# A layer's second output as seven block products with weight sums made in memory

## The reference, cut to what matters

```
h = rmsnorm(x, norm_ffn2) * (1 + sc3) + sh3
a, b = split(h @ w_in)            # w_in: 1024 x 5632
x = x + 0.5 * gt3 * (silu(a) * b) @ w_out     # g = silu(a) * b: 640 x 2816, w_out: 2816 x 1024
y = rmsnorm(x, norm_final)
```

## Time and profile before

| | |
|---|---|
| runs (us) | 1293.56, 1292.83, 1290.88 |
| profiled execution | span 1290.3 us; the page gives no whole time for it |
| TensorE busy | 1271.7 us of the span, 8909 matmuls |
| VectorE, ScalarE, POOL busy | 929.5, 553.6, 99.9 us |
| granted clock of TensorE | 0.999 of full in the mean |
| moved by DMA | 170.02 MB, mean 132 GB/s |

### The profile page before, as it was taken

The page is one execution under the profiler, slowest core; times in us unless marked ns, Lnnn a source line. Parts: engine busy times, 40 slices in busy tenths (PEclk is TensorE's granted clock), DMA queues, the critical chain, the costliest instruction groups (busy, mean ns, idle before and its releaser), DMA issues.

```text
span 1290.3 us, 23138 instructions
## 1 busy us (share of the span) xinstructions
PE 1271.7 (99%) x8909; PEld 1221.2 (95%) x8909; DVE 929.5 (72%) x1537; ACT 553.6 (43%) x920; POOL 99.9 (8%) x81
## 2 busy tenths in 40 slices
PE   9999999999999999999999999999999999999998
PEld 7889999999999999999999899999999999988886
DVE  5668877787887864666899867557988877771424
ACT  6514543445532224664433554336544343451223
POOL 0000000000000000002433663000000000000000
PEclk9999999999999999999999999999999999999999
DMA  9771423232476745348864552242243423274222
GB/s 372 296 271 31 117 78 98 69 94 63 142 219 189 217 119 142 89 116 192 246 201 100 146 157 83 66 71 78 66 129 97 142 72 98 65 185 103 71 83 98
DMA packets 238101, 170.02 MB, mean 132 GB/s; under 512 B 46305, under 2 KB 209606, under 8 KB 236998
## 3 DMA queue, kind: packets, MB, share of 16 engines
q1 hardware_dynamic: 234964, 165.51, 43.2%
q0 software_dynamic: 1440, 2.62, 1.5%
q10 hardware_dynamic: 1618, 0.81, 0.2%
HBM read 154.32 MB, written 19.83 MB: 135 GB/s over the span
## 4 chain that ended last, share of the span: by engine, by line
PE 80%; DVE 8%; DMA 5%; issue 3%; ACT 2%; POOL 2%; SPq 0%; POOLq 0%; DVEq 0%; ACTq 0%
PE ps L1043 32%; PE ps L850 26%; PE ps L1473 11%; PE ps L1420 3%; DMA d_ex<-d_gc 2%; PE ps L973 1%; DMA w_raw<-in_w_ffn_in 1%; PE ps L1406 1%; DVE cv L2513 1%; DVE w_lo L2109 1%; DVE sub_tmp L2633 1%; DMA cw_raw<-in_w_ada 1%; DVE pn L2178 1%; PE ps L918 1%; POOL Rc L3054 1%
## 5 line engine op out<-in xcount | busy, mean ns | idle before, releaser
L1512 ACT ACTIVATE w_hi<-w_raw 128x1024 fp32r<-128x1024 f32 (+1 forms) x101 | 105.1, 1041 | 308.2 <-PE ps L850 163.4
L2109 DVE TENSOR_TENSOR w_lo<-w_raw,w_hi 128x1024 fp32r<-128x1024 f32 (+1 forms) x101 | 125.5, 1243 | 126.5 <-ACT w_hi L1512 124.4
L850 PE MATMUL ps<-h_hi,w_hi 128*128 128x320 f32 x736 | 171.8, 315 | 0.7 <-DVE w_lo L2109 0.6
L850 PE MATMUL ps<-h_lo,w_hi 128*128 128x320 f32 x736 | 169.5, 311 | 0.0
L850 PE MATMUL ps<-h_hi,w_lo 128*128 128x320 f32 x736 | 169.2, 311 | 0.0
L850 PEld LDWEIGHTS ps<-h_hi,w_hi 128*128 128x128 f32 x736 | 123.6, 189 | 5.1 <-issue 4.9
L1043 PE MATMUL ps<-T_hi,S_hi 128*128 128x320 f32 x408 | 126.0, 309 | 0.0
L1043 PE MATMUL ps<-T_hi,S_lo 128*128 128x320 f32 x408 | 126.0, 309 | 0.0
L1043 PE MATMUL ps<-T_lo,S_hi 128*128 128x320 f32 x408 | 125.9, 309 | 0.0
L850 PEld LDWEIGHTS ps<-h_hi,w_lo 128*128 128x128 f32 x736 | 124.6, 189 | 0.0
L850 PEld LDWEIGHTS ps<-h_lo,w_hi 128*128 128x128 f32 x736 | 124.3, 189 | 0.0
(11 more groups left out here) (393 smaller groups left out, 2896.3 us busy)
## 6 DMA issues: line engine op xcount, KB each, us to landing
w_raw<-in_w_ffn_in SPq DMA_DIRECT2D x50, 512.0 KB, 4.8
cw_raw<-in_w_ada SPq DMA_DIRECT2D x40, 512.0 KB, 4.3
w_more<-in_w_ffn_in SPq DMA_DIRECT2D x34, 512.0 KB, 4.9
ada_w<-in_w_ada SPq DMA_DIRECT2D x16, 1024.0 KB, 8.8
w_raw<-in_w_ffn_out SPq DMA_DIRECT2D x30, 512.0 KB, 3.8
w_raw<-in_w_mix_in SPq DMA_DIRECT2D x28, 512.0 KB, 4.5
w_raw<-in_w_ffn_out SPq DMA_DIRECT2D x16, 448.0 KB, 3.9
w_raw<-in_w_mix_out SPq DMA_DIRECT2D x8, 512.0 KB, 3.8
```

The source lines that it names most:

```text
L850: last = pe.matmul(to[a_slot][b], w, m[:, k0 + k, part[b]], start=start and k == 0 and n == 0, stop=stop and k == kt - 1 and n == 2)
L1512: nc.scalar.activation(w_hi[:, slot, 0:kt * P], w_raw[:, slot, 0:kt * P], ACT.Copy).then_inc(hi_ready, 1)
L2109: nc.vector.tensor_tensor(w_lo[:, slot, 0:kt * P], w_raw[:, slot, 0:kt * P], w_hi[:, slot, 0:kt * P].bitcast(F32), ALU.subtract).then_inc( ...
```

## The change

The 16 first rows of w_out are taken as two halves of eight (A: rows 0 to 7, B: rows 8 to 15), the columns as two halves, and the four tiles of the second group as two pairs. The eight products of these blocks become seven: four over the first rows (`four`), two in the first half of the columns (`left`), one in the second (`right`), with sums of g and sums of w_out as operands. Three of the block results are added into others on VectorE (`combine`, `residual_rows`, `fold`). The first tile and rows 16 to 21 (`plain`) are multiplied as before.

The sums of g are made by VectorE in eight steps of the second input (`s_sums`, in the hook behind the steps that turn x), into the room of x. The four sums of w_out, eight blocks of 256 KB each, are made in memory (`d_ws`) by 64 transfers that POOL issues during the first output, 32 of them accumulating. POOL starts a block of sixteen when units 0, 6, 12 and 18 of the first output are done, and waits out each of its six waves.

w_out is loaded in 84 pieces of one row and 512 columns (256 KB) into a ring of eight; the split parts have a ring of four. gb is fetched behind piece 10, yo in five groups of four copies behind pieces 12, 14, 16, 18 and 20, nf_b behind piece 69.

```diff
 def load_out_rows():                                  # SP
-    for q in range(2 * UPC):
-        c, i = divmod(q, UPC)
-        sp.wait_ge(lo_ready, U_F2O + q - 1)
-        sp.dma_start(w_raw[:, q % 2, :]..., w_out_v[1][:, 2 * i:2 * i + 2, OW * c:OW * c + OW])
-        if q == 2:
...
-        if 3 <= q < 3 + NC:
-            for b in range(4): sp.dma_start(yo[32 * b:32 * b + 32, q - 3, :]..., view(d_xb...))
+    sp.wait_ge(st_rows, 16 * (GROUPS_DN + 2 + KD + 2))
+    for i in range(2):
+        sp.wait_ge(ws_in[i], WS_IN)
+    for n in range(R_ALL):
+        if n == 4:
+            sp.wait_ge(pr_done, LAST + 5)
+        if n == 6:
+            sp.wait_ge(*c12_rdy(SE[1] - 1))
+        if n >= 8:
+            sp.wait_ge(*lo_of(n - 8))
+        row, c, made = w_block(n)
+        src = w_out_v[1][:, row, OW * c:OW * c + OW] if made is None else d_ws[made, row]
+        sp.dma_start(w_raws[n % 8][:, :], src).then_inc(fr_in[n % 8], 16)
+        if n == 10:
...
+        if n >= 12 and n % 2 == 0 and (n - 12) // 2 < NC:
+            t = (n - 12) // 2
+            for b in range(4): sp.dma_start(yo[32 * b:32 * b + 32, t, :]..., view(d_xb...))

+def four(k):                                          # TensorE; a stripe is 3 matmuls
+    for j, (i, banks) in enumerate(((0, BX), (3, BY), (1, BZ), (2, BW))):
+        p = p_four(k, j)
+        pe.wait_ge(*lo_of(p))
...
+        for a in range(2):
+            last = stripe(p, banks[a], *block_rows(k, i, a, lows[j]), start=k == 0, stop=k == NH - 1)
+        last.then_inc(fo_mm, 1)

+def s_sums(i):                                        # VectorE, second input
...
+    if part == 0:
+        nc.vector.tensor_tensor(s1, a21, a22, ALU.subtract).then_inc(ps_rdy, 1)
+        nc.vector.tensor_tensor(s2, s1, a11, ALU.subtract).then_inc(ps_rdy, 1)
+    else:
+        nc.vector.tensor_tensor(a21, a11, a21, ALU.subtract).then_inc(ps_rdy, 1)
+        if step < 2:
+            nc.vector.tensor_tensor(s4[0][:, top, :], g32[:, low, P:3 * P], s2, ALU.add).then_inc(ps_rdy, 1)

+def weight_sums(i):                                   # POOL
+    ks = (2 * i, 2 * i + 1)
+    def added(j, k, row, c):
+        pool.dma_start(d_ws[j, k], w_out_p[:, row, OW * c:OW * c + OW], accum_op=ALU.add).then_inc(ready, 16)
+    for k in ks:
+        for j in (0, 2):
+            pool.dma_start(d_ws[j, k], w_out_p[:, k, OW:D]).then_inc(ready, 16)
+    pool.wait_ge(ready, n + 16 * 4)
+    for k in ks:
+        added(0, k, NH + k, 1)
+        added(2, k, k, 0)
+    pool.wait_ge(ready, n + 16 * 8)
+    for k in ks:
+        pool.dma_start(d_ws[1, k], d_ws[0, k]).then_inc(ready, 16)
...
+for i in range(NH // 2):
+    pool.wait_ge(mm_done, U_F1O + 6 * i + 1)
+    weight_sums(i)
 pool.wait_ge(st_rows, 16 * (GROUPS_DN + 2))
 for m in range(NC):
     if m > 0:
-        pool.wait_ge(in_sum, 32 * m)
+        pool.wait_ge(in_sum, WS_IN + 32 * m)
```

More of the change, by code:

```diff
@@ L331, in hybrid_layer @@
         d_gate = nc.dram_tensor("d_gate", [2, D], F32).ap()
+        d_ws = nc.dram_tensor("d_ws", [4, NH, P, OW], F32).ap()
         def twin(name, shape, at, size):
@@ L1457, in _, with stripe @@
             strassen(1)
[L1459 to L1474, removed]
-                return last
+            def stripe(p, bank, gh, gl, start=False, stop=False, f0=0, f1=OW):
+                wh, wl = (w[p % 4][:, f0:f1] for w in (ring_hi, ring_lo))
+                for n, (g, w) in enumerate(((gh, wh), (gl, wh), (gh, wl))):
+                    last = pe.matmul(ps[bank][:, 0:f1 - f0], g, w, start=start and n == 0, stop=stop and n == 2,
+                                     skip_group_check=True)
+                return last
@@ new lines, in right @@
+            def right(k):
+                p = p_right(k, 0)
+                pe.wait_ge(*lo_of(p))
+                if k == 0:
+                    pe.wait_ge(fe_rdy, FE + 6)
+                stripe(p, BY[1], *first_tile(k, 0), start=k == 0).then_inc(fo_mm, 1)
+                pe.wait_ge(*lo_of(p + 1))
+                if k % 4 == 0:
+                    pe.wait_ge(*rows_of(4 * NH + NPL + k // 4))
+                stripe(p + 1, BY[1], *first_tile(k, 1))
+                for a in range(2):
+                    last = stripe(p + 1, BW[a], *block_rows(k, 2, a, s4_lo[k // 4][:, k % 4, :]))
+                last.then_inc(fo_mm, 1)
@@ L1493, in _ @@
[L1493 to L1497, removed]
+            for k in range(NH):
+                four(k)
+            for k in range(NH):
+                left(k)
+            for r in range(NPL):
+                pe.wait_ge(*lo_of(p_plain(0, r)))
+                pe.wait_ge(*rows_of(4 * NH + r))
+                for t in range(NC):
+                    last = plain(0, t, r, stop=r == NPL - 1)
+                    if r == NPL - 1 and t < NC - 1:
+                        last.then_inc(oc_done, 1)
+                last.then_inc(fo_mm, 1)
@@ new lines, in _ @@
+            for k in range(NH):
+                right(k)
+            for r in range(2):
+                pe.wait_ge(*lo_of(p_plain(1, r)))
+                for t in range(NC):
+                    if r == 0 and t >= 3:
+                        pe.wait_ge(*out_read(t - 3))
+                    last = plain(1, t, r, start=r == 0 and t >= 3, stop=r == 1 and t == NC - 1)
+                last.then_inc(fo_mm, 1)
+            for r in (2, 3):
+                pe.wait_ge(*lo_of(p_plain(1, r)))
+                for t in range(2):
+                    plain(1, t, r)
@@ L2985, in second_half, with combine @@
                                                in1=nf_b[:, OW:], op0=ALU.mult, op1=ALU.mult).then_inc(r_rdy, 1)
[L2987 to L2996, removed]
+            def combine(out, a, one, two, op, step, *ready):
+                dve.wait_ge(*ready)
+                if step > 1:
+                    dve.wait_ge(fe_rdy, FE + 2 * step - 3 + a)
+                nc.vector.tensor_tensor(out[a][:, :], one, two, op).then_inc(fe_rdy, 1)
```

394 lines of the change are left out of this document (345 added, 49 removed).

## The result

The changed kernel takes 1315.99 us in the median of four runs (1314.13 to 1316.16) against 1292.61 (1290.88 to 1293.56) for the kernel before, measured beside it: ratio 1.0177, 95% interval [1.0163, 1.0191]. It is 23.4 us slower, where 6.6 were forecast, and the time lies 3 us above the range. The profiled execution spans 1314.1 us, 23.8 above the one before.

What follows compares the result with a forecast made beforehand. TensorE was taken to bound the kernel, with load latency on SP's queue also binding in the first output. Terms -10.9 + 9.5 + 2 + 0 + 6 = +6.6 us on 1292.8 gave 1299.4, range 1288 to 1313.

Steps and rivals of the forecast that it cites:

- Matmuls: Second output: 48 fewer matmuls of 512 columns on TensorE, 10.9 us less.
- SP's order: Second output: yo copies in fours hold SP's queue, so weight pieces leave late; 9.5 us more, ends 4.5 and 14.
- hand-over: Second output, after the four products: TensorE waits for ScalarE's copies and VectorE's sums; 2 us more, ends 0 and 4.
- Sums of g: Second input: one or two more VectorE operations a step fit beside TensorE; nothing, at most 1 us.
- Weight sums in memory: First output: POOL's transfers run beside it from 332 to 544 and delay w_ada loads; 6 us more, ends 0 and 16.
- With 1.5 more each: First output, after 411: w_ada loads 1.5 us longer, a column group 21.7 for 19.4, last two groups some 2 late each.
- The wait of 0.56: First output at 411.49: TensorE waits behind two w_ada loads without slack; 1 to 3.2 us more each, 2 to 6 together.
- The upper end, 16: First output: 16 us if each of 18 loads between 395 and 458 were late by 0.9, nothing covered.
- The price of a transfer: Weight sums: 5.1 to 8.9 us each by the rows, 8.8 a wave, 53 a block; the skill's 2.6 not followed.
- A: Rival, second output: copies do not hold SP, a group takes 2.8 us, the 9.5 go; 1289.9 or 1286; chance 0.20.
- B: Rival, first output: it absorbs the weight-sum transfers; 1293.4, no change; chance 0.16.
- C: Rival, mixer: POOL comes late to d_ex if a block exceeds 61 us; at 66 a block, 1314; chance 0.12.

Runs made afterwards that it cites:

- e3: The changed kernel with one residual yo copy behind every second weight piece, twenty times, instead of four copies five times: 1310.88 us.
- e12: The changed kernel with its weight sums beside the first input instead of the first output, yo copies still in fours: 1295.94 us.
- e2: The kernel before, with all 64 weight-sum transfers added beside its first output and used by nobody: 1313.97 us, ratio 1.0177.
- e6: The kernel before with only the first two of four blocks of unused weight sums beside its first output: 1307.11 us.
- e7: The kernel before with the 64 unused transfers beside its first output, all as plain copies without accumulation: median 15.6 us above the kernel before.
- e8: The kernel before with two blocks of unused weight sums beside its first output, each of 32 transfers awaited before the next: 1304.65 us.
- e1: The changed kernel with its weight sums moved behind the mixer, into the second input: 1311.4 us, ratio 1.015.
- e5: The changed kernel with yo copies one by one and weight sums beside the first input: 1287.65 us, ratio 0.9955.
- e9: The kernel before with all unused weight sums beside its first output and 30 w_ada loads cut to 128 columns: 5.5 us above e10, first output 162.3.
- e10: The kernel before with 30 of 32 w_ada loads cut to 128 columns and no weight sums: first output 160.5 us.
- f2: The changed kernel with yo copies one by one and no weight sums, pieces loaded from w_ffn_out itself: 1284.36 us, ratio 0.993.
- f1: The kernel before with weight sums beside its first input, used by nobody: 1293.83 us, ratio 1.0011.

## Why the prediction was wrong, by its own steps

*Matmuls, SP's order, hand-over: right in sum.* Forecast -10.9 + 9.5 + 2 = +0.6, measured +0.9. The 512-column matmuls are 600. SP's order cost 8.9 by e3 and 7.4 by e12 (forecast 9.5). What is left of the stage, 142.0 against 150.0 - 10.9 = 139.1, is 2.9: in e3 1.2 lies around two waits of 0.2 and 0.4 where the left products begin (hand-over, forecast 2), and 1.7 is pace, 0.2297 us for a matmul that took 0.2268, in no term. In the change the form was off: not four waits of 2 to 3 us but two of 1.9 and 1.8 and one of 0.6, with some 3.3 us lost to lower clock behind them; e12, at full clock, comes near the form that was forecast. With its pieces the first group of copies held SP for 8.4 us rather than 5.4, the others for 4.3 to 4.9: 27.3 in all, the forecast 27, by the luck of the parts.

*Sums of g: right.* The second input is as long as before.

*Weight sums in memory: the step that failed.* The blocks ran from 333 to 520, nearly without a pause as forecast, and the extra time of a load was right too: "With 1.5 more each", measured (169.3 - 127.5) / 30 = 1.4. What failed is the sentence "Two of them stand in the chain that already makes TensorE wait at 411", and charging "some 2 us late for each of the last two groups". A load goes out only when the sum two before it is done, so every one of the 30 loads stands in that chain, from 347 on: in the profiles before and after, all but the first leave within 0.3 us of that sum. Where no load has slack, each pair of them adds what one lands later: 15 x 1.4 = 20.9. The stage got 18.2 longer; its last column sum ended 16.7 later, and lower clock behind it cost 1.4. The same sum by the landings of the others: e2 21.6 (19.9 measured), e6 13.4 (9.6), e7 18.6 (18.7), e8 8.6 (6.5), and nothing for e1, e5 and e12, whose first output is unchanged; so up to 4 us of the sum were taken up. There was slack for it: 17 of the 30 column sums of the change start as their load lands, 11 before, the others later. e6 to e8 ran before this rule was put down, e9 and e10 behind it. The prediction had the chain's pace, 21.7 for 19.4, but for two groups; for the six to which its 32 loads at 5.3 a group belong, 2.3 each would have made 14. The wait of 0.56 was read as one tight place; it was the one place where a chain that ran beside the whole stage came to the surface. The upper end, 16, was built from the same 18 loads "between 395 and 458" and so was too low.

*The clock: in no term.* Some 7 of the 18.2 us are matmuls at a lower granted clock behind waits, the other 11 are waits (11.8 for 0.6). Where the next wait is for a load anyway, as at 416, a faster TensorE would only have waited longer, so this need not be 7 us on top of the chain of loads; no run separates the two. Behind the last wait (484 to 492, clock 0.82) it is 0.18 x 8 = 1.4, paid in full.

The price of a transfer was not the fault. The Trainium skill's fit, weighed in the prediction from "DMA: Bandwidth & Descriptors", section on the anatomy of one DMA on the GpSimd path, gives an estimate of 2.6 us for 256 KB. The trace agrees only nearly, and only where copies inside d_ws ran in twos (2.7 to 3.4 in e1's second input); in the first output the 46 that read w_ffn_out took 5.7 in the median, and the rows decide.

*Mixer: 4.1 us that no term held.* 1.8 of it is TensorE's delay behind ScalarE's late copy, which only kernels with accumulated sums show. The rest lies about the loads behind d_ex; by f2 it can be the execution's own variation.

*Rivals.* A fell: each group of copies held SP for 4.3 us or more, where it wanted under 3, and e12 shows the price. B fell: the first output absorbed nothing but the slack above. C did not happen: a block took 43 to 49 us, under its 61, and POOL still waited for d_gc. Its time, 1314, came near, by another way.

## What to carry to other kernels

Loads that wait for the use of the load two before them are a chain through the whole stage, even where the engine they feed hides it: price anything that slows them by up to (loads / buffers) x (extra landing), here 0.7 to 1.0 of it, not by the places where a wait already shows. Put background transfers beside loads that have a full step of lead; the same 64 transfers cost 20 us beside the first output, 8 to 13 beside the second input, and beside the first input nothing in that stage and 2 to 3 us much later (f1's median: 1.0, interval -0.6 to 3.6). A transfer in many short runs belongs one at a time between the loads on its queue, not in a burst.

## What the runs showed of the hardware that was not expected

- Plain copies in memory delayed the loads beside them nearly as much as accumulations: 18.7 us of first output for 19.9, in one profile each, though they landed in 4.5 us for 5.7. A w_ada load of an eighth of the size still took 4.1 us beside the sums, 1.9 without.
- Behind TensorE waits of 1.9 and 1.8 us the mean granted clock was 0.60 and 0.57 over the next 4 us or so; behind one of 4.0 us it was 0.61 over 7 us. Behind e12's four waits of 1.6 to 2.3 us, and one of 1.7 in e9's first output, it stayed at 1.00.
- A copy of yo goes out in 0.3 to 0.5 us alone (e3); of four in a row the third held SP for 1.5 to 3.4 us (the change).
- The five waves of accumulations into d_ex took 38.2 to 44.1 us from first issue to last landing in 16 profiles, with the same code for them, and the mixer 425.5 to 434.8; the one does not settle the other (f1: 41.7 and 430.5).
- In the nine profiles with accumulated weight sums ahead of the mixer, all landed over 300 us earlier, ScalarE's copy in the second input started 1.8 to 3.4 us after TensorE's last matmul for it; with no sums ahead of the mixer 0.04 in six, with plain copies 0.45 in one.
